# Two halves of a transposed row block placed between matmuls one by one, and the activation split moved ahead of the next weights at one seam of a two-block kernel

## The chip, the cores and the metric

The program runs on one core of one Trainium2 chip. The metric is the device time of one execution in microseconds (us). The engines are named as in the profile: PE is the matrix engine (PEld its weight loads), DVE the vector engine, ACT the scalar engine, POOL and SP the two others; SP issues the weight transfers.

## The reference

The input x is 256 tokens by 1024 columns. Two blocks follow each other, each of depth 2, all in float32:

```
# first block, for l in range(2)
proj = x @ w_in[l]                      # retention, mLSTM, gates
y_ret, y_ml = ..., ...                  # two sequence mixers, each with its own projection
mix = (gate_a * y_ret + gate_b * y_ml) @ w_out[l]
x = layer_norm(ALPHA * x + mix, ln1_g[l], ln1_b[l])
gu = x @ w_gate_up[l]
hidden = silu(gu[..., :D_FF]) * gu[..., D_FF:]
x = layer_norm(ALPHA * x + hidden @ w_down[l], ln2_g[l], ln2_b[l])

# second block, for l in range(2)
proj = rms_norm(h, norm_gain[l]) @ w_in_2[l]      # h starts as the x of the first block
y = ...                                           # dilated attention, stick-breaking attention, a gated recurrence
h = h + y @ w_out_2[l]
return rms_norm(h, final_gain)
```

Every projection needs the normalized activation with its columns on the partitions, while the normalization leaves it with tokens on the partitions. So after each normalization the kernel transposes the whole 256 by 1024 activation on PE.

## The kernel before, in words

**Split operands.** Each float32 product is made of three matmuls in a reduced float32 type: high weight by high activation, low weight by high, high weight by low. A weight unit is four blocks of 128 rows by 512 columns. SP loads it into `raw`; ACT copies it to `wh` (line 937, the high part); DVE subtracts to get `wl` (line 1362 for a unit or its second half, line 1373 for its first half alone). Rings of four `wh` and four `wl` buffers run ahead of PE. The activation is split in the same way: `xh` by ACT (line 973) and `xl` by DVE (line 1448), both read from the PSUM bank that PE transposed into, half of the 1024 columns at a time.

**Order.** There is no scheduler. Each engine has its program written out by hand, in the order of the projections (`mv0`, `mv1`, ..., `out0`, `out1`, `ff0`, ..., `dn1`, then `q`, `k`, ..., `o1` in the second block). Each engine works through its list in that order and waits on semaphores. On PE almost every matmul is issued from the helper at line 463; transposes of the normalized activation are at line 596.

**The seams.** The last projection ahead of a normalization is run by `by_half`: it first finishes token half t = 0 and then t = 1, so that the normalization of t = 0 lies beside the matmuls of t = 1. The normalized rows of t = 0 are transposed by `turn_x` between the last matmuls of t = 1. Behind it `pair` runs two projections together: t = 0 of both first, then t = 1; within the second one's first unit, at its third 128-row block (kk = 2), `turn_x` transposes the rows of t = 1. `turn_x` has two column halves, q = 0 and q = 1, each of four 128 by 128 transposes into one bank, and each waits for its half of the normalized row. `pair` meets its third unit in two halves on DVE: line 1373 makes the first half of `wl` before the normalization of t = 1 and line 1362 the second half behind it; PE waits for the second half at kk = 2.

In the first block this happens at `out1` and the pair `ff0`/`ff1` in both layers, and at `dn1` of layer 0 and the pair `mv0`/`mv1` of layer 1. **The passage** from the first block to the second is `dn1` of layer 1, followed by the pair `q`/`k`. There the rows pass two normalizations: X (lines 1621 to 1659, a layer norm), then squares on ACT (line 1100), a root on POOL (line 418) and the scaled rows `sg` (line 1642), which are transposed. In the second block the pair `q`/`k` of layer 1 follows the projection `o0`/`o1`, which calls `turn_x` for t = 0 in one piece before and after the change.

Of the kernel before, what the change touches and what calls it, by code (L numbers as in the profile page):

```python
# [13 lines left out]
P = 128  # L14
S = 256
D = 1024
DEPTH = 2
# [4 lines left out]
ALPHA = (2 * DEPTH) ** 0.25  # L22
LN_EPS = 1e-5
# [185 lines left out]
def program(nc, A, out):  # L209
# [8 lines left out]
    with top:  # L218
# [13 lines left out]
        X = sb("X", [P, 2, D])  # L232
# [220 lines left out]
        def tensor(pe):  # L453
# [90 lines left out]
            def half_k(t, bank, lh, ll, ready, k, unit, last, mid=None, mid_at=2):  # L544
                u, nk, h_, l_ = unit
                for kk in range(nk):
                    if mid and kk == mid_at:
                        mid()
                    if t == 0 and kk in (0, nk // 2):
                        pe.wait_ge(s_lo, 2 * u + 1 + (kk > 0))  # L550
                    ready(k + kk, t)
                    r = tok3(bank[:, :], lh, ll, k + kk, t, h_[:, kk, :], l_[:, kk, :], k + kk == 0)
                if t == 1:
                    r.then_inc(s_used, 1)
                elif last:
                    r.then_inc(s_half, 1)

            def by_half(name, l, head, tail, lh, ll, ready, mid, mid_at=3):
                k = 0
# [30 lines left out]
            def turn_x(l, tag, t, v, src, seen):  # L590
                for q in range(2):
                    name = f"{tag}{t}{q}"
                    bank, fill = open_aux(name, l)
                    pe.wait_ge(seen, v + 2 * t + q + 1)
                    for g in range(4):
                        r = pe.transpose(bank[:, tok_half(g)], src[:, P * (4 * q + g):P * (4 * q + g) + P], ident)  # L596
                    r.then_inc(fill, 1)
# [138 lines left out]
            for l in range(DEPTH):  # L736
                xw = x_whole(2 * l)
                one = lambda name, lh, ll, ready, mode, nu=2: group(SIDE1, steps, name, l, nu, lh, ll, ready, mode)
                if l == 0:
                    one("mv0", xh, xl, xw, "tok", 5)  # L740
                    one("mv1", xh, xl, xw, "tok")
                else:
                    pair("mv0", "mv1", l, x_part(2), lambda: turn_x(0, "xb", 1, 4, X[:, 1, :], s_xn), nothing, nothing)
# [15 lines left out]
                by_half("out1", l, 0, 2, mxh, mxl, mix_ready(l), lambda: turn_x(l, "xa", 0, 8 * l, X[:, 0, :], s_xn))  # L759
                pair("ff0", "ff1", l, x_part(2 * l + 1), lambda: turn_x(l, "xa", 1, 8 * l, X[:, 1, :], s_xn),  # L760
# [4 lines left out]
                if l == 0:  # L765
                    by_half("dn1", l, 4, 2, hdh, hdl, hidden_ready(l), lambda: turn_x(0, "xb", 0, 4, X[:, 0, :], s_xn), 3)
                else:
                    by_half("dn1", l, 3, 3, hdh, hdl, hidden_ready(l), lambda: turn_x(1, "xb", 0, 0, xn(0), s_rm), 2)
# [135 lines left out]
            for l in range(DEPTH):  # L904
                tag, at = ("xb", 1) if l == 0 else ("2x", 0)
                one = lambda name, mode: group(SIDE2, steps2, name, l, 2, xh, xl, x_whole(4 + l), mode)
                pair("q", "k", l, x_part(4 + l), lambda: turn_x(at, tag, 1, 4 * l, xn(1), s_rm), nothing, nothing)
# [5 lines left out]
                project(l, nothing if l == DEPTH - 1 else lambda: turn_x(0, "2x", 0, 4, xn(0), s_rm))  # L913
            assert use == NU

        def scalar(act):
# [186 lines left out]
            def by_half(name, l, head, tail, evac, mid):  # L1103
# [6 lines left out]
                for i in range(tail):  # L1110
                    if i == tail - 1:
                        mid()
                    highs(use - tail + i + 1 + RING)
# [29 lines left out]
            for l in range(DEPTH):  # L1143
# [35 lines left out]
                else:  # L1179
                    by_half("dn1", l, 3, 3, lambda t: squares(t, 4, [(s_xn, 12 + 2 * t + c + 1) for c in range(2)]),  # L1180
                            lambda: split_x("xb", l, 0, 4))
# [159 lines left out]
        def vector(dve):  # L1341
# [345 lines left out]
            def by_half(name, l, head, tail, evac, mid):  # L1687
# [9 lines left out]
                evac(0)  # L1697
                lows(high)
# [3 lines left out]
                mid()  # L1702
# [61 lines left out]
            for l in range(DEPTH):  # L1764
# [32 lines left out]
                by_half("dn1", l, 4 - l, 2 + l, lambda t: normal(l, "dn1", t, ALPHA, LN_EPS, 2 * l + 2), lambda: split_x("xb", l, 0, 2 * l + 2))  # L1797
# [209 lines left out]
```

## Time and profile before

| | |
|---|---|
| time, median of 3 runs | 1179.17 us (1177.88 to 1179.58) |
| profiled execution, its own time | 1179.37 us |
| span of the profiled execution | 1177.5 us |
| PE busy | 1160.3 us (99% of the span) |
| DVE, ACT, POOL busy | 741.8, 570.4 and 26.2 us |

The span runs from the first to the last instruction of the profile; 1.9 us of the time lie around it. The ends of matmuls are modelled by the profiler and overlap, so on PE the starts are what can be compared: a row's start less the start of the row ahead of it.

### The profile page before, as it was taken

The page shows a single profiled execution, that of the slowest core. Times are in us where ns is not written, and L with a number is a line of the kernel's source. Part 1 is how long each engine was busy: PE and PEld are TensorE (multiplying, and loading weights), DVE is VectorE, ACT ScalarE, POOL GpSimd, SP SyncE. Part 2 cuts the span into 40 slices and gives each one's busy share as a digit, 9 for nine tenths or more (in the row PEclk, how much of TensorE's full clock was granted, in tenths as well). Part 3 has the DMA queues.
Part 4 walks back from the last instruction along what each step waited for, and adds up shares of the span by engine and source line. Part 5 has one row for each costly group of instructions (what it writes and reads, how often), then busy time and mean ns, then how long its engine had stood idle before and what let it go on. Part 6 is the DMA issues. An engine that isn't in the chain of part 4 may idle for free.

```text
span 1177.5 us, 18016 instructions
## 1 busy us (share of the span) xinstructions
PE 1160.3 (99%) x7546; PEld 1042.4 (89%) x7546; DVE 741.8 (63%) x994; ACT 570.4 (48%) x658; POOL 26.2 (2%) x36
## 2 busy tenths in 40 slices
PE   8999999999999999999999999999999899999997
PEld 6988998998999988998998898899988689978995
DVE  5877556667655546686764667755545666775674
ACT  5563445442544434454444534444432556845673
POOL 0000000001000000000000000000000000000000
PEclk9999999999999999999999999999999999999999
DMA  9664454556665563745545556665566363336420
GB/s 343 220 215 144 144 181 176 180 186 201 224 212 190 167 212 112 250 151 172 170 144 189 179 179 214 230 208 182 169 203 208 125 215 128 127 138 243 137 80 36
DMA packets 129871, 211.45 MB, mean 180 GB/s; under 512 B 6528, under 2 KB 52608, under 8 KB 129664
## 3 DMA queue, kind: packets, MB, share of 16 engines
q1 hardware_dynamic: 128048, 204.02, 51.9%
q0 software_dynamic: 1744, 6.29, 1.8%
q8 instruction: 60, 0.98, 0.3%
q14 instruction: 19, 0.16, 0.0%
HBM read 209.24 MB, written 1.05 MB: 179 GB/s over the span
## 4 chain that ended last, share of the span: by engine, by line
PE 89%; DVE 5%; ACT 3%; DMA 2%; issue 1%; SPq 0%; POOL 0%; DVEq 0%; POOLq 0%; ACTq 0%
PE ps L463 85%; DMA raw<-in_w_in 2%; DVE wl L1362 1%; ACT wh L937 1%; PE ps L656 1%; PE ps L691 1%; PE ps L794 0%; DVE mqk L1490 0%; PE ps L596 0%; ACT sg L1100 0%; ACT xh L973 0%; DVE sg L1642 0%; PE ps L776 0%; PE ps L663 0%; DVE yl L1832 0%
## 5 line engine op out<-in xcount | busy, mean ns | idle before, releaser
L1362 DVE TENSOR_TENSOR wl<-raw,wh 128x2048 fp32r<-128x2048 f32 (+1 forms) x190 | 424.0, 2237 | 180.0 <-ACT wh L937 179.6
L937 ACT ACTIVATE wh<-raw 128x2048 fp32r<-128x2048 f32 (+1 forms) x190 | 359.9, 1900 | 181.0 <-PE ps L463 166.1
L463 PE MATMUL ps<-xh,wh 128*128 128x256 f32 x1200 | 337.1, 282 | 0.0
L463 PE MATMUL ps<-xl,wh 128*128 128x256 f32 x1200 | 332.1, 277 | 0.0
L463 PE MATMUL ps<-xh,wl 128*128 128x256 f32 x1184 | 328.4, 277 | 0.0
L463 PEld LDWEIGHTS ps<-xh,wh 128*128 128x128 f32 x1200 | 225.9, 188 | 3.2 <-issue 2.4
L463 PEld LDWEIGHTS ps<-xl,wh 128*128 128x128 f32 x1200 | 226.0, 188 | 0.4
L463 PEld LDWEIGHTS ps<-xh,wl 128*128 128x128 f32 x1184 | 222.6, 188 | 0.0
L463 PE MATMUL ps<-wh,xh 128*128 128x512 f32 (+1 forms) x512 | 203.8, 398 | 4.7 <-DVE wl L1362 2.4
L463 PE MATMUL ps<-wh,xl 128*128 128x512 f32 (+1 forms) x512 | 196.9, 385 | 0.0
L463 PE MATMUL ps<-wl,xh 128*128 128x512 f32 (+1 forms) x512 | 196.7, 384 | 0.0
L463 PEld LDWEIGHTS ps<-wh,xh 128*128 128x128 f32 x512 | 96.7, 189 | 26.8 <-DVE wl L1362 4.8
L463 PEld LDWEIGHTS ps<-wh,xl 128*128 128x128 f32 x512 | 96.5, 188 | 19.7
L463 PEld LDWEIGHTS ps<-wl,xh 128*128 128x128 f32 x512 | 96.8, 189 | 17.4
L463 PE MATMUL ps<-wh,hdh 128*128 128x512 f32 x176 | 68.7, 390 | 0.0
L463 PE MATMUL ps<-wl,hdh 128*128 128x512 f32 x176 | 68.5, 389 | 0.0
L463 PE MATMUL ps<-wh,hdl 128*128 128x512 f32 x176 | 68.5, 389 | 0.0
L1092 ACT ACTIVATE tmp<-ps 128x512 f32<-128x512 f32 x18 | 10.8, 598 | 63.5 <-PE ps L463 63.5
L463 PEld LDWEIGHTS ps<-wh,hdl 128*128 128x128 f32 x176 | 33.0, 188 | 6.9
L463 PEld LDWEIGHTS ps<-wh,hdh 128*128 128x128 f32 x176 | 33.0, 188 | 6.7
L463 PEld LDWEIGHTS ps<-wl,hdh 128*128 128x128 f32 x176 | 33.1, 188 | 6.7
L418 POOL TENSOR_TENSOR small<-small,cst 128x1 f32<-128x1 f32 (+1 forms) x18 | 17.9, 994 | 897.0 <-DVE small L1650 392.3
(259 smaller groups left out, 1384.6 us busy)
## 6 DMA issues: line engine op xcount, KB each, us to landing
raw<-in_w_in SPq DMA_DIRECT2D x90, 1024.0 KB, 5.1
raw<-in_w_gate_up SPq DMA_DIRECT2D x88, 512.0 KB, 4.9
raw<-in_w_down SPq DMA_DIRECT2D x20, 1024.0 KB, 4.9
raw<-in_w_out SPq DMA_DIRECT2D x16, 1024.0 KB, 5.0
raw<-in_w_proj_ret SPq DMA_DIRECT2D x8, 1024.0 KB, 4.9
raw<-in_w_proj_mlstm SPq DMA_DIRECT2D x8, 1024.0 KB, 5.0
rows<-in_ln_g POOLq DMA_DIRECT2D x4, 512.0 KB, 4.3
rows<-in_ln_b POOLq DMA_DIRECT2D x4, 512.0 KB, 5.7
```

What stands on the lines that cost most here:

```text
L418: pool.tensor_tensor(o, in_, C("mhalf", 0, n), ALU.pow).then_inc(after, 1)
L463: return pe.matmul(o, a, b, start=start, stop=False, skip_group_check=True)
L656: r = pe.matmul(bank[:, 0:257], dd_of(h)[:, o:o + P], mv[:, s, h, 0:257], start=(s == 0), stop=(s == t))
L691: r = pe.transpose(bank[:, S * k2 + P * t:S * k2 + P * t + P], src[:, t, tok_half(k)], ident)
L937: act.activation(stretch(wh, u, 0, m), source(u)[:, 0:m], ACT.Copy).then_inc(s_hi, 1)
L1092: act.activation(a_[:, :], main(name, l)[0][:, :], ACT.Silu).then_inc(freed_by(name, l, 0), 1)
L1362: dve.tensor_tensor(stretch(wl, u, a, nk * n), source(u)[:, a:nk * n], f32(stretch(wh, u, a, nk * n)), ALU.subtract).then_inc(s_lo, 1 if a ...
```

## The change

`turn_x` now does one column half, and `half_k` calls it twice: q = 0 ahead of block `mid_at`, q = 1 ahead of the next block, or behind the last block if there is no next one. In `by_half` of the first three seams q = 0 moves one block forward and q = 1 stays; in all pairs q = 0 stays and q = 1 moves one block back. At the passage both move back: q = 0 by one block, q = 1 to behind the last matmul of `dn1`. At the passage alone, ACT copies one weight unit instead of two before it makes `xh`, and DVE makes `xl` ahead of the next `wl` instead of behind it.

```diff
             def half_k(t, bank, lh, ll, ready, k, unit, last, mid=None, mid_at=2):
                 u, nk, h_, l_ = unit
                 for kk in range(nk):
-                    if mid and kk == mid_at:
-                        mid()
+                    if mid and kk - mid_at in (0, 1):
+                        mid(kk - mid_at)
                     if t == 0 and kk in (0, nk // 2):
                         pe.wait_ge(s_lo, 2 * u + 1 + (kk > 0))
                     ready(k + kk, t)
...
                 elif last:
                     r.then_inc(s_half, 1)
-
-            def by_half(name, l, head, tail, lh, ll, ready, mid, mid_at=3):
+                if mid and mid_at == nk - 1:
+                    mid(1)
+
+            def by_half(name, l, head, tail, lh, ll, ready, mid, mid_at=2):
...
-            def turn_x(l, tag, t, v, src, seen):
-                for q in range(2):
-                    name = f"{tag}{t}{q}"
-                    bank, fill = open_aux(name, l)
-                    pe.wait_ge(seen, v + 2 * t + q + 1)
-                    for g in range(4):
-                        r = pe.transpose(bank[:, tok_half(g)], src[:, P * (4 * q + g):P * (4 * q + g) + P], ident)
-                    r.then_inc(fill, 1)
+            def turn_x(l, tag, t, v, src, seen, q):
+                bank, fill = open_aux(f"{tag}{t}{q}", l)
+                pe.wait_ge(seen, v + 2 * t + q + 1)
+                for g in range(4):
+                    r = pe.transpose(bank[:, tok_half(g)], src[:, P * (4 * q + g):P * (4 * q + g) + P], ident)
+                r.then_inc(fill, 1)
...
-                    by_half("dn1", l, 4, 2, hdh, hdl, hidden_ready(l), lambda: turn_x(0, "xb", 0, 4, X[:, 0, :], s_xn), 3)
+                    by_half("dn1", l, 4, 2, hdh, hdl, hidden_ready(l), lambda q: turn_x(0, "xb", 0, 4, X[:, 0, :], s_xn, q))
                 else:
-                    by_half("dn1", l, 3, 3, hdh, hdl, hidden_ready(l), lambda: turn_x(1, "xb", 0, 0, xn(0), s_rm), 2)
+                    by_half("dn1", l, 3, 3, hdh, hdl, hidden_ready(l), lambda q: turn_x(1, "xb", 0, 0, xn(0), s_rm, q), 3)
...
-            def by_half(name, l, head, tail, evac, mid):
+            def by_half(name, l, head, tail, evac, mid, mid_after=None):
...
-                    if i == tail - 1:
+                    if i == (tail - 1 if mid_after is None else mid_after):
                         mid()
...
-                            lambda: split_x("xb", l, 0, 4))
+                            lambda: split_x("xb", l, 0, 4), 1)
...
-            def by_half(name, l, head, tail, evac, mid):
+            def by_half(name, l, head, tail, evac, mid, mid_first=False):
...
                 evac(0)
+                if mid_first:
+                    mid()
                 lows(high)
                 for i in range(tail - 1):
                     lows(high)
                     highs(use - tail + i + 1 + RING)
-                mid()
+                if not mid_first:
+                    mid()
                 raise_high(use + RING)
                 first_half_low()
```

The first place is DVE at the passage, before and then after: `sg` is the scaled row of t = 0, `xl` its low part, `wl` the low part of weights, `X<-X,ps` the first step of the normalization of t = 1.

```order
L1642 SCALAR_TENSOR_TENSOR sg<-X,small,rows 128x512
L1362 TENSOR_TENSOR wl<-raw,wh 128x2048 [waits s_hi]
L1448 TENSOR_TENSOR xl<-ps,xh 128x4x128 [waits s_xh,s_fill2]
L1448 TENSOR_TENSOR xl<-ps,xh 128x4x128 [waits s_xh,s_fill3]
L1373 TENSOR_TENSOR wl<-raw,wh 128x1024 [waits s_hi]
L1621 SCALAR_TENSOR_TENSOR X<-X,ps 128x512 [waits s_used]
```

```order
L1642 SCALAR_TENSOR_TENSOR sg<-X,small,rows 128x512
L1448 TENSOR_TENSOR xl<-ps,xh 128x4x128 [waits s_xh,s_fill2]
L1448 TENSOR_TENSOR xl<-ps,xh 128x4x128 [waits s_xh,s_fill3]
L1362 TENSOR_TENSOR wl<-raw,wh 128x2048 [waits s_hi]
L1373 TENSOR_TENSOR wl<-raw,wh 128x1024 [waits s_hi]
L1621 SCALAR_TENSOR_TENSOR X<-X,ps 128x512 [waits s_used]
```

The whole `wl` unit went from ahead of the two `xl` to behind them; all six still stand ahead of the normalization of t = 1.

The second place is PE in the pair `q`/`k` behind the passage, at blocks kk = 2 and kk = 3 of k's first unit, before and then after; `cst` is the identity, and `[waits s_lo]` is the wait for the second half of that unit's `wl`.

```order
L596 MATMUL ps<-cst,sg 128x128 [waits s_rm,s_drain0]
L596 MATMUL ps<-cst,sg 128x128 x3
L596 MATMUL ps<-cst,sg 128x128 [waits s_rm,s_drain1]
L596 MATMUL ps<-cst,sg 128x128 x3
L463 MATMUL ps<-wh,xh 128x512 [waits s_lo]
L463 MATMUL ps<-wl,xh 128x512
L463 MATMUL ps<-wh,xl 128x512
L463 MATMUL ps<-wh,xh 128x512
```

```order
L596 MATMUL ps<-cst,sg 128x128 [waits s_rm,s_drain0]
L596 MATMUL ps<-cst,sg 128x128 x3
L463 MATMUL ps<-wh,xh 128x512 [waits s_lo]
L463 MATMUL ps<-wl,xh 128x512
L463 MATMUL ps<-wh,xl 128x512
L596 MATMUL ps<-cst,sg 128x128 [waits s_rm,s_drain1]
L596 MATMUL ps<-cst,sg 128x128 x3
L463 MATMUL ps<-wh,xh 128x512
```

Four of the eight transposes went from ahead of the wait for the weights to three matmuls behind it. The other pairs have the same order, with `X` in place of `sg` in the first block.

The third place is PE at the end of `dn1` at the passage, after the change: the three `hdh`/`hdl` rows are block kk = 3, the last of `dn1`, and the row with `xh` is the first matmul of `q`.

```order
L596 MATMUL ps<-cst,sg 128x128 [waits s_rm,s_drain2]
L596 MATMUL ps<-cst,sg 128x128 x3
L463 MATMUL ps<-wh,hdh 128x512
L463 MATMUL ps<-wl,hdh 128x512
L463 MATMUL ps<-wh,hdl 128x512
L596 MATMUL ps<-cst,sg 128x128 [waits s_rm,s_drain3]
L596 MATMUL ps<-cst,sg 128x128 x3
L463 MATMUL ps<-wh,xh 128x512 [waits s_drain2,s_lo,s_free0]
```

Before, all eight transposes stood ahead of block kk = 2, with six matmuls between them and `q`.

## Rows read from the trace of the kernel before

**Rows 1.** The page, part 1: busy us (share of span) and instructions.
```profile
PE 1160.3 (99%) x7546; PEld 1042.4 (89%) x7546; DVE 741.8 (63%) x994; ACT 570.4 (48%) x658; POOL 26.2 (2%) x36
```

**Rows 2.** Waits of PE: us in total, times, longest us.
```profile
PE ps L463 <- DVE wl L1362: 2.4, 3, 1.5
PE ps L596 <- DVE sg L1642: 2.2, 2, 1.7
PE ps L463 <- DVE xl L1448: 2.1, 4, 0.8
```

**Rows 3.** Timeline, out1 of layer 0: start, us, engine, what [idle before].
```profile
277.08 1.41 DVE L1659 SCALAR_TENSOR_TENSOR X<-X,small,rows 128x512 f32<-128x512 f32 x2
...
278.56 1.03 PE L596 MATMUL ps<-cst,X 128*128 128x128 f32 x8
279.20 1.09 ACT L973 ACTIVATE xh<-ps 128x512 fp32r<-128x512 f32 x2 [0.50 <-PE ps L596]
...
279.89 1.29 DVE L1448 TENSOR_TENSOR xl<-ps,xh 128x512 fp32r<-128x512 f32 x2 [1.40 <-ACT xh L973]
...
280.73 0.47 PE L463 MATMUL ps<-wh,xh 128*128 128x512 f32 x1 [0.44 <-DVE xl L1448]
```

**Rows 4.** Timeline, pair ff0/ff1 of layer 0.
```profile
286.64 1.22 DVE L1362 TENSOR_TENSOR wl<-raw,wh 128x1024 fp32r<-128x1024 f32 x1
...
287.66 1.03 PE L596 MATMUL ps<-cst,X 128*128 128x128 f32 x8
...
288.45 0.48 PE L463 MATMUL ps<-wh,xh 128*128 128x512 f32 x1
...
289.91 0.39 PE L463 MATMUL ps<-wh,xh 128*128 128x512 f32 x1
```

**Rows 5.** Timeline at the passage, end of dn1 to start of q.
```profile
914.26 3.70 ACT L937 ACTIVATE wh<-raw 128x2048 fp32r<-128x2048 f32 x2
...
915.46 1.42 DVE L1642 SCALAR_TENSOR_TENSOR sg<-X,small,rows 128x512 f32<-128x512 f32 x2 [0.73 <-POOL small L418]
915.48 0.39 PE L463 MATMUL ps<-wh,hdl 128*128 128x512 f32 x1
...
916.35 1.29 PE L596 MATMUL ps<-cst,sg 128*128 128x128 f32 x8 [0.49 <-DVE sg L1642]
916.79 2.29 DVE L1362 TENSOR_TENSOR wl<-raw,wh 128x2048 fp32r<-128x2048 f32 x1
...
918.99 1.28 DVE L1448 TENSOR_TENSOR xl<-ps,xh 128x512 fp32r<-128x512 f32 x2
...
919.82 0.47 PE L463 MATMUL ps<-wh,xh 128*128 128x512 f32 x1 [0.80 <-DVE xl L1448]
...
920.19 1.21 DVE L1373 TENSOR_TENSOR wl<-raw,wh 128x1024 fp32r<-128x1024 f32 x1
...
921.32 0.68 DVE L1621 SCALAR_TENSOR_TENSOR X<-X,ps 128x512 f32<-128x512 f32 x1
```

**Rows 6.** Timeline in the pair q/k behind the passage.
```profile
928.57 1.29 PE L596 MATMUL ps<-cst,sg 128*128 128x128 f32 x8 [1.69 <-DVE sg L1642]
...
930.27 0.79 PE L463 MATMUL ps<-wh,xh 128*128 128x512 f32 x1 [0.41 <-DVE wl L1362]
...
930.87 0.63 PE L463 MATMUL ps<-wl,xh 128*128 128x512 f32 x1
...
932.57 0.63 PE L463 MATMUL ps<-wh,xl 128*128 128x512 f32 x1
```

**Rows 7.** Windows: stretch, us, busy by engine (x), PEclk, DMA share, GB/s.
```profile
930.00:931.00 1.00, 0.72 (x2) 0.63 (x3) 1.00 (x3) 0.49 (x1) 0.00 (x0) 0.50 0.33 49
...
933.00:934.00 1.00, 1.00 (x5) 0.85 (x4) 0.62 (x1) 0.00 (x0) 0.00 (x0) 0.83 0.93 285
```

**Rows 8.** Timeline, pair q/k of layer 1 of the second block.
```profile
1054.57 1.03 PE L596 MATMUL ps<-cst,sg 128*128 128x128 f32 x8
...
1055.75 0.19 PEld L463 LDWEIGHTS ps<-wh,xh 128*128 128x128 f32 x1 [0.39 <-DVE wl L1362]
```

More of the change, by code:

```diff
@@ L742, in tensor @@
                 else:
-                    pair("mv0", "mv1", l, x_part(2), lambda: turn_x(0, "xb", 1, 4, X[:, 1, :], s_xn), nothing, nothing)
+                    pair("mv0", "mv1", l, x_part(2), lambda q: turn_x(0, "xb", 1, 4, X[:, 1, :], s_xn, q), nothing, nothing)
                 gate(l)
@@ L758, in tensor @@
                 one("out0", mxh, mxl, mix_ready(l), "tok")
-                by_half("out1", l, 0, 2, mxh, mxl, mix_ready(l), lambda: turn_x(l, "xa", 0, 8 * l, X[:, 0, :], s_xn))
-                pair("ff0", "ff1", l, x_part(2 * l + 1), lambda: turn_x(l, "xa", 1, 8 * l, X[:, 1, :], s_xn),
+                by_half("out1", l, 0, 2, mxh, mxl, mix_ready(l), lambda q: turn_x(l, "xa", 0, 8 * l, X[:, 0, :], s_xn, q))
+                pair("ff0", "ff1", l, x_part(2 * l + 1), lambda q: turn_x(l, "xa", 1, 8 * l, X[:, 1, :], s_xn, q),
                      lambda: hidden_turn(l, 0, 0), lambda: hidden_turn(l, 0, 1))
@@ L906, in tensor @@
                 one = lambda name, mode: group(SIDE2, steps2, name, l, 2, xh, xl, x_whole(4 + l), mode)
-                pair("q", "k", l, x_part(4 + l), lambda: turn_x(at, tag, 1, 4 * l, xn(1), s_rm), nothing, nothing)
+                pair("q", "k", l, x_part(4 + l), lambda q: turn_x(at, tag, 1, 4 * l, xn(1), s_rm, q), nothing, nothing)
                 one("av", "tok")
@@ L912, in tensor @@
                 values_and_gates(l)
-                project(l, nothing if l == DEPTH - 1 else lambda: turn_x(0, "2x", 0, 4, xn(0), s_rm))
+                project(l, nothing if l == DEPTH - 1 else lambda: [turn_x(0, "2x", 0, 4, xn(0), s_rm, q) for q in range(2)])
             assert use == NU
@@ L1796, in vector @@
                 one("dn0", lambda: first_columns(l, "dn0", ALPHA), 6)
-                by_half("dn1", l, 4 - l, 2 + l, lambda t: normal(l, "dn1", t, ALPHA, LN_EPS, 2 * l + 2), lambda: split_x("xb", l, 0, 2 * l + 2))
+                by_half("dn1", l, 4 - l, 2 + l, lambda t: normal(l, "dn1", t, ALPHA, LN_EPS, 2 * l + 2), lambda: split_x("xb", l, 0, 2 * l + 2), l == 1)
             def rope(l):
```

## The prediction

> **What bounds the kernel now.** I read the page first: PE is busy 1160.3 of 1177.5 us [rows 1], so time can only be won in PE's few gaps or by taking work off PE, and the change takes none off. The waits of PE come next: three of them belong to the seams the change touches, 2.4 us for `wl`, 2.2 us for `sg` and 2.1 us for `xl` [rows 2]. The timelines then show where they lie. The four waits for `xl` are 0.80 us at the passage [rows 5] and three times about 0.44 us, one of them at `out1` of layer 0 [rows 3]; 0.80 + 3 x 0.44 is the 2.1 us. The waits for `sg` are 0.49 us ahead of the transposes of t = 0 [rows 5] and 1.69 us ahead of those of t = 1 [rows 6]. Everything outside these seams is matmul after matmul and is not touched.
>
> **Prices.** Eight transposes take PE 287.66 to 288.45, 0.79 us, so four take 0.40 us. A warm 512-column matmul takes 0.23 us: 30 of them lie between 280.73 and 287.66 [rows 3, 4]. The six behind the eight transposes take 1.46 us instead of 1.38 [rows 4], so a return from transposes to matmuls costs 0.08 us, and each half that is set apart costs 0.48 us of PE in place of 0.40. The hops are: first transpose to `xh` 0.64 us, `xh` to `xl` 0.69, `xl` to the matmul that needs it 0.84 [rows 3].
>
> **The three seams of the first block, t = 0.** At `out1`, the first half of X is ready in the middle of the two L1659, at 277.79. PE saw `sg` 0.18 us after its first half was ready (915.46 + 0.71 to 916.35) [rows 5], so q = 0 could start at 277.97, close to where kk = 2 started (278.56 less 3 x 0.23 = 277.87). Then 0.48 + 0.69 + 0.48 + 0.69 brings PE to 280.31. The data side is ready earlier, at 277.97 + 0.64 + 0.69 + 0.84 = 280.14. PE starts the next projection at 280.31 instead of 280.73: 0.42 us won.
>
> **The pairs behind them, t = 1.** The gain meets the next wait. PE would come to the transposes at 287.24, do four until 287.72, and then need the second half of `wl`, which DVE finishes at 286.64 + 1.22 = 287.86 [rows 4]. Before, the eight transposes covered that to the end. DVE gets to it through the normalization of t = 1, which starts no earlier: DVE's second `xl` ends where it did (277.97 + 1.17 for the second transposes, + 0.64 + 0.69 = 280.47, against 279.89 + 0.60 = 280.49). So kk = 2 starts at about 287.9, then 0.69 + 0.1 for the restart, 0.48, 0.69: the t = 1 pass starts at 289.8 instead of 289.91. Of 0.42 us about 0.1 is left. The third seam and the one in layer 1 show the same waits, so I take 3 x 0.1 = **-0.3 us**, with bounds of -1.3 (3 x 0.42 kept) and +0.3 (nothing won, three more returns at 0.08).
>
> **The passage, t = 0.** PE issued the last matmul of kk = 1 at 915.48 and then stood for `sg`. Now kk = 2 comes first, and q = 0 starts at 915.48 + 4 x 0.23 = 916.40, q = 1 at 916.40 + 0.48 + 0.69 = 917.57. `xh` starts at 917.04 and 918.21 (ACT is free, since one weight copy of 1.85 us from 914.26 ends at 916.1 [rows 5]), `xl` at 917.73 and 918.90. So `q` starts at 917.73 + 0.84 = 918.57 instead of 919.82: 1.25 us won on PE for the moment.
>
> DVE pays for it. Before, it went from `sg` (916.88) straight through `wl`, both `xl` and half of the next `wl` to X at 921.32, without a gap [rows 5]: `wl` filled the time in which transposes and `xh` were made. Now it waits from 916.88 to 917.73 and again between the two `xl`. The starts follow: `wl` at 918.90 + 0.60 = 919.50, the half `wl` 2.20 us later (918.99 less 916.79) at 921.70, X 1.13 us later (921.32 less 920.19) at 922.83. The normalization of t = 1 starts **1.51 us** later. PE first meets the late `wl`: 12 matmuls from 918.57 end at 921.3 and `wl` ends at 919.50 + 2.29 = 921.8, half a microsecond of waiting. Then it runs out of matmuls before the transposes of t = 1, and these wait for the chain from X, which took 921.32 to 928.57 [rows 5, 6] and is not shortened: they start at 930.08 instead of 928.57. The wait of 1.69 us becomes about 3.8. The won 1.25 us is swallowed in it, and the 1.51 us remain. Bounds: 0 below, since DVE had no idle time to give back and X cannot start before 921.32; 1.9 above, if each of the two DVE waits is 0.2 us longer (the hop of `sg` to PE again).
>
> Rows and a rule can be weighed here. At `out1` DVE stood idle for 1.40 us before `xl` although the weights of the next operation were there [rows 3]: a waiting instruction keeps those behind it back. The Trainium skill, TensorE: Matmul & The Clock Gate, section "Architectural detail", says the same of DVE and ACT, strict first in, first out. A DVE that let `wl` pass the waiting `xl` would make this term 0 and the time 1180.0; row and rule give 1181.5.
>
> **The passage, t = 1.** Before, all eight transposes lay in the time in which the second half of `wl` was made; PE went on when that was there, at 930.27 [rows 6]. Now four of them come three matmuls later, with nothing to hide them: **+0.48 us**, at the low clock more like 0.9; at the least 0.
>
> **The pair q/k of layer 1.** Here too PE waited 0.39 us for the second half of `wl` behind the eight transposes [rows 8]. Four move out of the covered time: **+0.48 us**, or 0 if they found cover. Its t = 0 part is unchanged.
>
> **Sum.** -0.3 + 1.51 + 0.48 + 0.48 = +2.2 us on the profiled execution's own 1179.37 us (span 1177.5 and 1.9 around it): **1181.5 us**. The profiled execution lies 0.2 us above the median, less than the terms' uncertainty. SP's loads and the copies behind the late `wl` are off the path: the weights they refill are used a whole ring later.
>
> **The clock.** Behind the two waits of rows 6 the granted clock stood at 0.50, the lower level of 1.2 GHz, and came back during the microsecond from 933 (0.83: a third of it low) [rows 7]. Matmuls went at (932.57 - 930.87) / 4 = 0.425 us; from 930.27 to 933.34 these are seven, 0.195 us dearer each, 1.4 us in all. That loss is in the time before; I keep it the same after.
>
> **Rivals.**
> 1. The clock stays low longer. PE's first wait more than doubles and a second of 1.2 us follows it, so the low stretch may begin earlier and outlast the restart by more, or the transposes run in it. Price up to another 1.4 us: 1182.9. It decides if the matmuls after the restart are slow for more than 3.1 us. The Trainium skill's same page, part 1, says that the low rate is the default and that activity lifts it, which speaks for it; that the low stretch ended while PE worked without a pause [rows 6, 7] agrees.
> 2. The clock doesn't fall. The four transposes now break the wait at another point. 1181.5 - 1.4 = 1180.1. The fastest run before, 1177.88, lies 1.3 us under the median, about this price, so such executions may exist; against it, the wait is longer.
> 3. The seams' gains are kept in full: 1181.5 - 1.0 = 1180.5. It needs the second half of `wl` 0.3 us earlier in the pairs, and DVE's chain gives no reason.
> 4. The 1.25 us at the passage are kept. It needs X to start at 921.32 or before and the chain behind it to have slack: 1179.37 - 1.25 - 0.3 + 0.48 = 1178.3. The rows speak against it, DVE being full from 915.46 to 921.32.
> 5. The order doesn't matter, because the halves reach `xh` together anyway: 1179.4. The order of the instructions speaks against it.
>
> **How the numbers follow.** Chances: my forecast 0.49 (1180.8 to 1182.3), clock longer 0.20, clock up 0.13, seams in full 0.08, passage kept 0.07, nothing 0.03. Dropping the far tails leaves 1178.6 to 1183.5. A measurement of this kernel can tell about 0.2%, 2.36 us, from no change; against the median that is 1181.5, where my forecast stands. Half of it and rival 1 are slower: 0.43. The other half with rivals 2 to 5 is no change: 0.53. Faster needs rival 4 with rivals 2 and 3 on top, 1175.9: 0.04.
>
> **What would show it.** Right: in the profile after, the waits of 0.44 us for `xl` at the three seams are gone and new waits for `wl` of 0.1 to 0.3 us stand in the pairs; at the passage DVE is idle before each `xl`, X of t = 1 starts 7.4 us after the first `sg` of t = 0 instead of 5.9 (921.32 less 915.46), and PE's wait for the `sg` of t = 1 is near 3.8 us. Wrong: X of t = 1 starts no later relative to `sg` of t = 0, or the transposes of t = 1 are not what PE waits for.

## The result, and the profile after

The changed kernel takes **1185.53 us** (median of 10 executions, 1181.86 to 1191.06) against 1179.01 for the kernel before (10 executions, 1177.88 to 1179.58): a ratio of 1.0052, interval [1.0041, 1.0063]. It is slower, and by more than forecast: 1181.5 us was expected, and the measured median lies above the range, which ended at 1183.5 us. The single times are also spread over 9.2 us where those of before span 1.7. The profiled execution is the slowest of the ten, 1191.06 us, span 1189.2.

The page's busy time of PE, which answers to [rows 1], and the waits of PE (total us, times, longest us), which answer to [rows 2]:

```profile
PE 1169.5 (98%) x7546; PEld 1050.7 (88%) x7546; DVE 742.8 (62%) x994; ACT 570.7 (48%) x658; POOL 26.2 (2%) x36
```

```profile
PE ps L463 <- DVE wl L1362: 4.0, 8, 1.4
PE ps L596 <- DVE sg L1642: 3.9, 1, 3.9
PE ps L463 <- DVE xl L1448: 0.4, 1, 0.4
```

The waits moved as forecast: those for `xl` went from four to one, those for `wl` from three to eight, and those for `sg` are now one long one. Yet the three together grew by 1.6 us only, while PE is busy 9.2 us longer with the same 7546 instructions. So most of the loss is in no wait at all.

**Where it lies.** The 6800 main matmuls (line 463) come in the same order in both kernels, so their starts can be compared one by one. In the profiled execution the changed kernel has lost 1.4 us by the second projection, where it waits for the first weights (that differs by as much and more between the profiles of the other kernels, whose instructions are the same up to there); it wins 0.2 us at the three seams and pairs, loses **3.5 us in `ff2` to `ff10` of each layer**, 3.2 us at the passage and 0.4 us at the pair q/k of layer 1. Less some 0.15 us of smaller steps this is the 11.7 us by which the spans differ.

**The seams and pairs.** The timeline at `out1` and the pair behind it, where [rows 3, 4] are those of before:

```profile
278.39 1.41 DVE L1659 SCALAR_TENSOR_TENSOR X<-X,small,rows 128x512 f32<-128x512 f32 x2
...
279.29 0.63 PE L596 MATMUL ps<-cst,X 128*128 128x128 f32 x4
...
281.58 0.40 PE L463 MATMUL ps<-wh,xh 128*128 128x512 f32 x1
...
289.20 0.50 PE L463 MATMUL ps<-wh,xh 128*128 128x512 f32 x1 [0.20 <-DVE wl L1362]
...
290.00 0.60 PE L596 MATMUL ps<-cst,X 128*128 128x128 f32 x4
```

The matmul at 281.58 has no wait where that of before had 0.44 us, and the pair has the new wait for `wl`, 0.20 us.

**The ff stage.** In `ff2` to `ff10` the activation is what moves: 864 matmuls of 256 columns, one behind the other. The first matmul of the stage, three neighbours in the middle of it and the first of `dn0` behind it, in the changed kernel and then in the kernel before:

```profile
305.27 0.28 PE L463 MATMUL ps<-xh,wh 128*128 128x256 f32 x1
...
350.17 0.28 PE L463 MATMUL ps<-xh,wh 128*128 128x256 f32 x1
350.29 0.28 PE L463 MATMUL ps<-xl,wh 128*128 128x256 f32 x1
350.40 0.28 PE L463 MATMUL ps<-xh,wl 128*128 128x256 f32 x1
...
407.41 0.39 PE L463 MATMUL ps<-wh,hdh 128*128 128x512 f32 x1
```

```profile
304.06 0.28 PE L463 MATMUL ps<-xh,wh 128*128 128x256 f32 x1
...
350.30 0.28 PE L463 MATMUL ps<-xh,wh 128*128 128x256 f32 x1
350.42 0.28 PE L463 MATMUL ps<-xl,wh 128*128 128x256 f32 x1
350.53 0.28 PE L463 MATMUL ps<-xh,wl 128*128 128x256 f32 x1
...
402.66 0.40 PE L463 MATMUL ps<-wh,hdh 128*128 128x512 f32 x1
```

From first to last row this is 102.14 us against 98.60. No row has a wait, and no instruction is added: the matmuls start 117.8 ns apart instead of 113.3. (Two decimals of a microsecond cannot show this between neighbours; it is the mean over the last 816 of the stage.) This distance from start to start is called the pitch below. The granted clock is not the reason. The windows of the changed kernel (stretch, us, busy by engine, PEclk, DMA share, GB/s) show PE full and the clock at 1.00:

```profile
305.00:355.00 50.00, 50.00 (x426) 49.92 (x425) 26.64 (x20) 22.68 (x20) 0.00 (x0) 1.00 0.68 219
```

In this window PE starts 426 matmuls; in the same 50 us of before it starts 442.

**The passage**, where [rows 5, 6] are those of before:

```profile
923.57 1.41 DVE L1642 SCALAR_TENSOR_TENSOR sg<-X,small,rows 128x512 f32<-128x512 f32 x2 [0.72 <-POOL small L418]
...
925.84 0.69 DVE L1448 TENSOR_TENSOR xl<-ps,xh 128x512 fp32r<-128x512 f32 x1 [0.85 <-ACT xh L973]
...
926.67 0.47 PE L463 MATMUL ps<-wh,xh 128*128 128x512 f32 x1 [0.44 <-DVE xl L1448]
...
926.97 0.69 DVE L1448 TENSOR_TENSOR xl<-ps,xh 128x512 fp32r<-128x512 f32 x1 [0.44 <-ACT xh L973]
...
930.91 0.68 DVE L1621 SCALAR_TENSOR_TENSOR X<-X,ps 128x512 f32<-128x512 f32 x1
...
938.15 0.63 PE L596 MATMUL ps<-cst,sg 128*128 128x128 f32 x4 [3.87 <-DVE sg L1642]
...
939.86 0.80 PE L463 MATMUL ps<-wh,xh 128*128 128x512 f32 x1 [1.08 <-DVE wl L1362]
...
941.31 1.05 PE L596 MATMUL ps<-cst,sg 128*128 128x128 f32 x4
...
945.15 0.60 PE L463 MATMUL ps<-wl,xh 128*128 128x512 f32 x1
945.57 0.41 PE L463 MATMUL ps<-wh,xl 128*128 128x512 f32 x1
```

Reckoned from `sg`, `q` starts after 3.10 us instead of 4.36, X of t = 1 after 7.34 instead of 5.86, and the transposes of t = 1 after 14.58 instead of 13.11. DVE stands still for 0.85 and 0.44 us ahead of the two `xl`.

### The profile page after: what moved, and what is told of

Read it like the earlier page. It is cut to its first block, busy times and chain, and to the rows that moved or that the text cites. A ratio compares the mean times of both kernels' runs of the same rounds, so it can differ in the third digit from the quotient of the medians.

```text
span 1189.2 us, 18016 instructions
## 1 busy us (share of the span) xinstructions
PE 1169.5 (98%) x7546; PEld 1050.7 (88%) x7546; DVE 742.8 (62%) x994; ACT 570.7 (48%) x658; POOL 26.2 (2%) x36
## 4 chain that ended last, share of the span: by engine, by line
PE 87%; DVE 6%; ACT 2%; DMA 2%; issue 1%; SPq 0%; POOL 0%; DVEq 0%; POOLq 0%; ACTq 0%
PE ps L463 84%; DVE wl L1362 2%; DMA raw<-in_w_in 2%; PE ps L656 1%; ACT wh L937 1%; PE ps L596 1%; PE ps L691 1%; PE ps L794 0%; DVE X L1659 0%; DVE mqk L1490 0%; DVE wl L1373 0%; SPq L402 0%; DVE sg L1642 0%; PE ps L663 0%; PE ps L776 0%
```

## The experiments

Each diff is against the kernel before, cut to its core. For the pitch, the table behind the second group gives the distance of neighbouring starts between breaks.

**First: which part brings the 118 ns.** Four kernels, each with one part of the change.

The passage alone (PE, ACT and DVE as in the change; PE's part shown):

```diff
-                    by_half("dn1", l, 3, 3, hdh, hdl, hidden_ready(l), lambda: turn_x(1, "xb", 0, 0, xn(0), s_rm), 2)
+                    by_half("dn1", l, 3, 3, hdh, hdl, hidden_ready(l), lambda q: turn_x(1, "xb", 0, 0, xn(0), s_rm, q), 3)
```

> Only the passage is changed (both halves of t = 0 later at the end of dn1 of layer 1, ACT and DVE in the new order); all other seams and pairs stand as before. In the trace of the change ff2 to ff10 go at 118 ns a matmul instead of 113, 3.53 us more in each layer, and the passage costs some 3.15 us. Theory PHASE (the 118 ns come from the way in which PE enters the stage, so from the splits at out1 and the pair ff0/ff1): both ff stages here at 113 ns, 98.5 us from first to last start, and the time 1179.0 + 3.15 = 1182.2 us. Theory OUTSIDE (the pitch is a state of the execution or of the weight transfers, and any kernel can fall into it): 118 ns here too in some of the executions, single times of 1185.7 and 1189, as with the whole change. My forecast's terms for the passage alone, with the clock loss as before and k unsplit: 1179.0 + 1.5 = 1180.5 us. The waits as forecast: sg of t = 1 near 3.8 us.

Measured: 1181.25 us, ratio 1.0016 [1.0007, 1.0025]; ff at 113 ns in both layers, no time above 1182.11. PE's wait for `sg` of t = 1 is 3.83 us, X starts 7.34 us after `sg`. That is 1.8 us more than before in its set, where +1.5 was forecast. In the profiled execution the transposes of t = 1 come 1.47 us later, and 0.64 us of it came back because the clock rose sooner behind them. The passage brings no 118 ns.

The first block alone: seams and pairs as in the change, passage and q/k as before.

```diff
-                by_half("out1", l, 0, 2, mxh, mxl, mix_ready(l), lambda: turn_x(l, "xa", 0, 8 * l, X[:, 0, :], s_xn))
-                pair("ff0", "ff1", l, x_part(2 * l + 1), lambda: turn_x(l, "xa", 1, 8 * l, X[:, 1, :], s_xn),
+                by_half("out1", l, 0, 2, mxh, mxl, mix_ready(l), lambda q: turn_x(l, "xa", 0, 8 * l, X[:, 0, :], s_xn, q))
+                pair("ff0", "ff1", l, x_part(2 * l + 1), lambda q: turn_x(l, "xa", 1, 8 * l, X[:, 1, :], s_xn, q),
```

> Only the first block is changed: q = 0 one block earlier at out1 of both layers and dn1 of layer 0, q = 1 one block later in the three pairs; the passage and the pairs q/k stand as before. PHASE: the seams win 0.3 us as forecast, and the ff stages fall to 118 ns in one or both layers in many executions: 1178.7, 1182.2 or 1185.8 us, so a median near 1182 and a spread of several us where the kernel before has 1.7. OUTSIDE: the same spread could show, but it would show in the passage kernel as well. If the pitch comes with the passage or with the program's length, 1178.7 us without a spread. Passage: PE's wait for sg of t = 1 stays 1.7 us.

Measured: 1178.4 us, 0.9994 [0.9985, 1.0003], 113 ns in both layers, single times 1177.65 to 1179.92. By the trace the three seams with their pairs win 0.14 us together. No execution fell to 118 ns here, against what I had expected of PHASE; the third group comes back to it.

The three seams alone: the pairs call both halves ahead of kk = 2, as before.

```diff
-                by_half("out1", l, 0, 2, mxh, mxl, mix_ready(l), lambda: turn_x(l, "xa", 0, 8 * l, X[:, 0, :], s_xn))
+                by_half("out1", l, 0, 2, mxh, mxl, mix_ready(l), lambda q: turn_x(l, "xa", 0, 8 * l, X[:, 0, :], s_xn, q))
```

> Only the three seams are split (q = 0 one block earlier at out1 of both layers and dn1 of layer 0); all pairs do their eight transposes in one piece, as before. By the rows, PE comes 0.42 us earlier to the pair, and the eight transposes (0.79 us) cover the time until the second half of wl is there, so the gain is kept: 1179.0 - 3 x 0.42 = 1177.8 us if ff stays at 113 ns. PHASE: PE enters the ff stage at another instant but behind the same instructions; if the instant against the data side decides, 118 ns in some layers (+3.53 us each: 1181.3 or 1184.8); if the order of PE's last instructions decides, 113 ns and 1177.8. OUTSIDE: 1177.8 with a spread of 3.5 us steps.

Measured: 1177.69 us, 0.9990 [0.9981, 0.9999], 113 ns. By the starts each seam wins 0.49 to 0.55 us, and no pair waits for `wl`: the eight transposes cover it. This part of the change is worth having.

The pairs alone, with both halves in one piece at the seams, as before.

```diff
-                pair("ff0", "ff1", l, x_part(2 * l + 1), lambda: turn_x(l, "xa", 1, 8 * l, X[:, 1, :], s_xn),
+                pair("ff0", "ff1", l, x_part(2 * l + 1), lambda q: turn_x(l, "xa", 1, 8 * l, X[:, 1, :], s_xn, q),
```

> Only the three pairs of the first block are split (q = 1 one block later); the seams ahead of them stand as before. PE reaches the pair as before, four transposes last 0.48 us and the second half of wl is there 0.2 us after the first of them began, so no wait is new and only the second return from transposes to matmuls is added, 0.08 us each: 1179.0 + 0.25 = 1179.3 us if ff stays at 113 ns. PHASE: the pair's new order shifts PE's entry into ff2 by some nanoseconds: 118 ns in one or both layers, 1182.8 or 1186.3 us. OUTSIDE: 1179.3 us with steps of 3.5 us in single executions.

Measured: 1185.47 us, 1.0062 [1.0048, 1.0075], all five times from 1184.81 to 1188.4, and **118 ns in both layers**. Three transposed halves that move by three matmuls, with no wait added, cost 6 us in a stage 15 us further on (by the starts 7.1 us in the two stages; 1.4 us came back behind the passage, where the clock did not fall in the profiled execution).

**Second: the breaks.** In the ff stage of all these traces the pitch changes only behind the small transposes of the hidden rows, two 128 by 128 transposes that stand twice in `ff2`. A kernel with one break more was the test, first on the split pairs, then on the kernel before with nothing of the change.

```diff
+            def extra_turn(l, j, t):
+                bank, fill = open_aux(f"f{j}{t}", l)
+                main_done(f"ff{j}", l, t)
+                for k in range(2):
+                    pe.transpose(bank[:, tok_half(k)], tmp[2 + t][:, tok_half(k)], ident)
-    "ff2": (("f 1 0",), ("f 1 1",), (), ()),
+    "ff2": (("f 1 0",), ("x 1 1",), ("f 1 1",), ()),
```

> The kernel with only the pairs of the first block split went at 118 ns in ff2 to ff10 of both layers, 1185.47 us, and its trace changes pitch just behind the two small transposes that ff2 holds: 118 ahead of the first pair of them, 113 between, 118 behind the second. Here one further pair of the same transposes (into the same bank, written over by the next) stands in ff2, in both layers. PHASE (the pitch is carried from matmul to matmul and is set anew by each break in the row of matmuls): the third break sets it anew, most simply back to 113: 1185.5 - 7.0 + 2 x 0.3 for the added transposes = 1179.1 us; that it stays at 118 is possible too, since the kernel before shows a break that left it there. OUTSIDE (a state of the execution, or of the transfers, or of what this pair order loads): 118 all the same, 1185.5 + 0.6 = 1186.1 us.

Measured: 1186.9 us, 1.0068 [1.0056, 1.0080]; it stayed at 118.

> The kernel before, with nothing of the change, and the same further pair of small transposes in ff2 of both layers: four transposes in all. The trace of before has 118 ns ahead of and behind the first break and 113 behind the second. PHASE: the third break sets the pitch anew, and ff2 to ff10 go at 118 ns: 1179.3 + 2 x (3.5 + 0.3) = 1186.9 us. If so, the 7 us can be had without any part of the change. OUTSIDE: 113 as in before, 1179.3 + 0.6 = 1179.9 us.

Measured: 1186.6 us, 1.0062 [1.0050, 1.0074], and 118 ns in both layers. First matmul of `ff2` and first of `dn0` in its timeline:

```profile
305.96 0.28 PE L463 MATMUL ps<-xh,wh 128*128 128x256 f32 x1
...
408.32 0.39 PE L463 MATMUL ps<-wh,hdh 128*128 128x512 f32 x1
```

102.36 us: two transposes of some 0.2 us cost 3.8 us a layer. The loss can be had without the change.

These sequences suggested a cycle, and a fourth break on the split pairs tested it (`"x 1 1"` stands in two places of `ff2`):

```diff
-    "ff2": (("f 1 0",), ("f 1 1",), (), ()),
+    "ff2": (("f 1 0",), ("x 1 1",), ("x 1 1",), ("f 1 1",)),
```

> The pairs of the first block split, as in the kernel that gave 1185.47 us, with two further pairs of small transposes in ff2 instead of one, so four breaks in all. Read from four traces, each break of two transposes takes the row of matmuls one step on in a cycle of three, 118, 118, 113 and 118 again: the kernel before comes in at the first and has 118, 118, 113; with a further break 118, 118, 113, 118; the split pairs come in at the second and have 118, 113, 118; with a further break 118, 113, 118, 118. Theory CYCLE: here 118, 113, 118, 118, 113, so ff3 to ff10 go at 113 ns in both layers: 1185.5 - 2 x (3.5 - 0.7) = 1179.9 us, with 0.25 us for each added pair of transposes and some matmuls more at 118. Theory ORDER (the split pair order itself gives 118, and added transposes can only add): 118 behind the last break, 1185.5 + 4 x 0.25 = 1186.5 us.

Measured: 1180.23 us, 1.0011 [1.0002, 1.0019], 113 ns in both layers, 0.3 us from the forecast of CYCLE. Its two rows:

```profile
307.24 0.28 PE L463 MATMUL ps<-xh,wh 128*128 128x256 f32 x1
...
406.45 0.40 PE L463 MATMUL ps<-wh,hdh 128*128 128x512 f32 x1
```

99.21 us with two breaks more, where the same kernel with one more had 102.4. The mean distance of starts in each piece between breaks (from the tenth matmul of a piece on, the same in both layers):

| kernel | ns ahead of the first break, then behind each |
|---|---|
| before; seams alone; passage alone; first block alone (both sets) | 117.8, 117.8, **113.3** |
| before with one break more | 117.8, 117.8, 113.3, **117.8** |
| changed, profile of the result; pairs alone | 117.8, 113.3, **117.8** |
| changed, profiles of two further sets (third group) | 117.8, 117.8, **113.3** |
| pairs alone with one break more | 117.8, 113.3, 117.8, **117.8** |
| pairs alone with two breaks more | 117.8, 113.3, 117.8, 117.8, **113.3** |

Each break of two transposes takes one step in the cycle 118, 118, 113; the kernels differ in the step at which they come in. The last piece is 768 to 816 matmuls long, and 816 x 4.45 ns = 3.6 us.

**Third: the whole change again**, and beside it the first block alone.

> The whole change once more, beside the other kernels on one chip. Its PE does up to 912 us the same in the same order as the kernel with only the first block changed, which stood at 113 ns and 1178.4 us in all its executions. PHASE: which of the two it gets is decided by the nanosecond at which DVE's wl releases PE in the pair (445 ns from matmul to matmul there in the one, 468 in the other), so it can differ from execution to execution and from chip to chip: single times in groups near 1181.0, 1184.6 and 1188.1 us, for none, one or two layers at 118 ns, and the profiled one has the pitch that its time says. If the whole change fixes the pitch: all near 1185.5 to 1188.

Measured: 1185.98 us, 1.0059 [1.0039, 1.0079], times 1181.7, 1182.74, 1185.4, 1186.56, 1189.02 and 1189.93. The profiled execution is the one of 1181.7 us, and both its layers are at 113 ns. So the same program has both pitches.

> The kernel with only the first block changed again, now on the same chip as the whole change. It had 113 ns in all its executions (1177.65 to 1179.92 us), the whole change in the two other sets 113 or 118 from execution to execution, although PE does the same up to 912 us in both. CHIP (the release that decides falls differently on different chips, or from set to set): single times in groups near 1178.5, 1182 and 1185.5 us here too, or none in both kernels. KERNEL (something in the rest of the change moves that release by nanoseconds): all near 1178.5 us here, mixed in the whole change beside it.

Measured: 1179.61 us, 1.0011 [1.0001, 1.0022]; five of twelve times lie above all of before's in that set (1180.96 to 1184.7). The theory KERNEL, that this program always has 113, falls by these times alone: the profiled execution is at 113, and no profile caught this program at 118.

> The whole change beside the kernel with only the first block changed, on one chip. CHIP: the same mix of layers at 113 and 118 ns as there. KERNEL: single times in groups near 1181.5, 1185 and 1189 us again (so far 5, 8 and 3 of 16), while the other stays at 1178.5. In the profiled execution the release of PE by wl in the pair ff0/ff1, reckoned back from the first matmul of ff2, tells the pitch: 16.068 to 16.069 us back went with 118, 16.078 to 16.113 with 113 in six layers.

Measured: 1183.28 us, 1.0045 [1.0032, 1.0057], times 1182.56 to 1187.48; profiled the one of 1182.56, at 113 ns in both layers. Its release by `wl` lies 16.079 us ahead of `ff2` in both layers, on the side that the expectation gave to 113; no further profile at 118 came to test the other side.

The two kernels in whose pairs PE stands for `wl` between the two halves of the transposes are mixed, one of them by its times only; in the kernels without that wait every profile had the pitch of its row in the table.

The record has the same at a second place. Near 39 us PE waits for `hml`, does four small matmuls and then 96 matmuls of 256 columns in a row. PE's instructions up to there are the same in all kernels here, yet the row goes at 113 ns in nine of the 16 profiles and at 118 ns in seven. The second matmul of the row and the 89th behind it, in the kernel before and then with the pairs alone:

```profile
39.00 0.28 PE L463 MATMUL ps<-xl,wh 128*128 128x256 f32 x1
...
49.10 0.28 PE L463 MATMUL ps<-xh,wh 128*128 128x256 f32 x1
```

```profile
39.37 0.28 PE L463 MATMUL ps<-xl,wh 128*128 128x256 f32 x1
...
49.85 0.28 PE L463 MATMUL ps<-xh,wh 128*128 128x256 f32 x1
```

That is 10.10 us against 10.48. So the order of the instructions alone does not fix the pitch behind a wait. (Here it costs next to nothing: what the faster row wins, PE loses behind it in a wait for `gb`, 0.34 us in the kernel before.)

**Fourth: the passage and q/k, taken apart.** DVE in the old order, the rest of the passage as in the change, all other seams and pairs as before:

```diff
-                by_half("dn1", l, 4 - l, 2 + l, lambda t: normal(l, "dn1", t, ALPHA, LN_EPS, 2 * l + 2), lambda: split_x("xb", l, 0, 2 * l + 2), l == 1)
+                by_half("dn1", l, 4 - l, 2 + l, lambda t: normal(l, "dn1", t, ALPHA, LN_EPS, 2 * l + 2), lambda: split_x("xb", l, 0, 2 * l + 2))
```

(this one against the changed kernel.)

> Of the change only the passage, and there PE's two later halves and ACT's earlier xh, but DVE in the old order, wl ahead of both xl. With xl first as well the passage alone gave 1181.25 us, and X of t = 1 started 7.3 us after sg. Theory DVE (the idle of DVE ahead of each xl is what pushes the normalization of t = 1 back): X starts 5.9 us after sg again, xl ends where it did before, q starts as before, and PE's wait for sg of t = 1 is back near 1.7 us: 1179.4 us. Theory PE (the halves set apart on PE cost the time): the time stays near 1181 us, with the wait for sg unchanged at some 3.8 us.

Measured: 1179.58 us, 1.0007 [0.9998, 1.0016]. In its timeline, where the line numbers are 6 higher:

```profile
915.93 1.41 DVE L1648 SCALAR_TENSOR_TENSOR sg<-X,small,rows 128x512 f32<-128x512 f32 x2 [0.73 <-POOL small L418]
...
921.05 1.22 DVE L1379 TENSOR_TENSOR wl<-raw,wh 128x1024 fp32r<-128x1024 f32 x1 [0.31 <-ACT wh L943]
922.20 0.68 DVE L1627 SCALAR_TENSOR_TENSOR X<-X,ps 128x512 f32<-128x512 f32 x1
...
929.45 1.75 PE L596 MATMUL ps<-cst,sg 128*128 128x128 f32 x8 [2.07 <-DVE sg L1648]
```

X starts 6.27 us after `sg`: 1.07 of the 1.48 us are gone with DVE's order. Of the 0.41 us that are left beyond before, 0.31 stand in the row of `wl` as a wait for `wh`: ACT, which now copies one unit of weights instead of two ahead of `xh`, comes to it later. Theory DVE holds for the larger part, with a share for ACT that I had not named; the row shows it, no run changed ACT's order by itself.

The pairs q/k alone:

```diff
-                pair("q", "k", l, x_part(4 + l), lambda: turn_x(at, tag, 1, 4 * l, xn(1), s_rm), nothing, nothing)
+                pair("q", "k", l, x_part(4 + l), lambda q: turn_x(at, tag, 1, 4 * l, xn(1), s_rm, q), nothing, nothing)
```

> Only the pairs q/k of the second block are split, in both layers; all else as before. The forecast's two terms by themselves: 0.48 us in layer 1 and 0.48 to 0.9 us behind the passage, where the four transposes that have moved may run at the lower level of the clock: 1179.2 + 1.0 to 1.4 = 1180.2 to 1180.6 us. Rival (the moved transposes find cover, because the rows behind them were ready early): 1179.2 us. ff at 113 ns in both layers in any case, since nothing ahead of it is changed.

Measured: 1179.11 us, 1.0005 [0.9995, 1.0015]. The time alone is inconclusive, its interval holds both theories. By the starts the profiled execution, 1180.47 us, loses 0.66 us behind the passage and 0.43 us in layer 1 against that of before, together the 1.1 us by which the two differ. The clock fell behind the passage in both, at different moments, so the 0.66 us are not the split alone.

**Fifth: the other stage, and a faster kernel.** `yr0` to `ym1` went at 118 ns in all kernels so far. Seams alone, and the last four transposes of `hml` in two breaks of two:

```diff
-    "yr0": (("om 0",), ("om 1",), ("om 2",), ("om 3",)),
+    "yr0": (("om 0",), ("om 1",), ("om 2",), ("oma 3",)),
+    "yr1": (("om 3",), (), (), ()),
...
-                for k2 in range(2):
+                for k2 in part:
...
-                r.then_inc(fill, 1)
+                if 1 in part:
+                    r.then_inc(fill, 1)
```

> The kernel with the three seams split alone (1177.69 us), and in yr0/yr1 of both layers the last four transposes of hml set in two breaks of two, one in the last place of yr0 and one at the first place of yr1; no transpose is added. In all kernels so far yr0 to ym1 went at 118 ns behind four breaks of four. CYCLE: if a break of two takes a step here too, two of them lead from the first 118 through the second to 113, and some 290 matmuls a layer go 4.4 ns faster: 1177.7 - 2 x 1.2 = 1175.3 us. If breaks act otherwise in this stage (other operands in other places of memory): 118 as before, 1177.7 + 0.2 = 1177.9 us.

Measured: 1177.96 us, 0.9988 [0.9979, 0.9997], no better than the seams alone. The trace has 117.8 up to the first of the two breaks, 113.3 for 24 matmuls, and 117.8 behind the second: a step in the cycle each, but this stage comes in one step later than I had assumed. So four breaks of two are needed:

```diff
-    "yr0": (("om 0",), ("om 1",), ("om 2",), ("om 3",)),
+    "yr0": (("om 0",), ("om 1",), ("oma 2",), ("om 2",)),
+    "yr1": (("oma 3",), ("om 3",), (), ()),
```

> The three seams split alone, and in yr0/yr1 of both layers the last two groups of four transposes of hml each set in two breaks of two. With the last group alone so divided the trace went 118, 113 for 24 matmuls, and 118 again behind the second break: the stage comes in at the second step of the cycle, and breaks of four leave the pitch where it is. CYCLE: four breaks of two take it from the second step over 113, 118, 118 to 113, which then holds for some 240 matmuls a layer: 46.8 to about 45.9 us from first to last start of the stage, 2 x 0.9 us off the kernel with the seams alone (1177.69 us, 1177.96 with the last group divided): 1175.9 us. If the agreement so far was chance: 118 behind the last break, 1177.9 us.

Measured: **1174.39 us, 0.9960 [0.9948, 0.9973]**, faster than both kernels. First matmul of `yr0`, two neighbours behind the fourth break, and the first of `out0`:

```profile
210.39 0.28 PE L464 MATMUL ps<-orh,wh 128*128 128x256 f32 x1
...
240.20 0.28 PE L464 MATMUL ps<-omh,wl 128*128 128x256 f32 x1
240.31 0.28 PE L464 MATMUL ps<-omh,wh 128*128 128x256 f32 x1
...
256.29 0.40 PE L464 MATMUL ps<-wh,mxh 128*128 128x512 f32 x1
```

45.90 us, where the kernel before has 46.98 (210.41 to 257.39 in its timeline):

```profile
210.41 0.28 PE L463 MATMUL ps<-orh,wh 128*128 128x256 f32 x1
...
257.39 0.40 PE L463 MATMUL ps<-wh,mxh 128*128 128x512 f32 x1
```

The last 240 matmuls are at 113.3 ns in both layers. The time is 1.5 us below the forecast. By the starts the profiled execution is 3.6 us ahead of that of before: 1.5 us at the three seams and 2.2 us in the two stages, less 0.2 us at the clock behind the passage. The medians differ by 4.6 us; the rest I leave to the spread of five executions.

## Why the prediction was wrong

**The step that failed** is a sentence of the first part: "Everything outside these seams is matmul after matmul and is not touched." The ff stage is touched: it costs 3.53 us more in a layer that goes at 118 ns, 7.1 us in the two. In all profiles its pitch follows from the step of a cycle of three at which PE comes out of the pair ahead of it, and the pair was changed. In the first four experiments only split pairs gave 118 ns; the kernel before with one break more has it without any part of the change, so breaks alone move the pitch, and two breaks more on the split pairs bring 113 ns back. None of the five rivals had it, so the range missed too. What in the machine makes the cycle is not shown by any run.

**The rest of the sum held, but for the clock.** The two profiled executions of the changed kernel in which ff kept 113 ns took 1181.7 and 1182.56 us; the forecast was 1181.5. By the starts, with the first 63 us and the ff stage left out, the three profiles of this kernel lose 3.3, 2.6 and 3.4 us against before, where the sum had 2.2. The surplus lies at the clock behind the passage, below.

| term | forecast, us | measured by starts, us |
|---|---|---|
| three seams with their pairs | -0.3 | -0.19 (changed, three profiles), -0.14 and -0.16 (first block alone) |
| a seam by itself | -0.42 | -0.49 to -0.55 (seams alone) |
| passage, t = 0 | +1.51 | +1.47 (14.58 less 13.11) |
| passage, t = 1, with the clock behind it | +0.48 to 0.9, clock as before | +0.66 (q/k alone); +1.71, +0.91, +1.65 (changed, three profiles) |
| pair q/k of layer 1 | +0.48 | +0.41 to +0.45 |
| ff stage | 0 | 0 or 7.1 in the profiles |

**The seams.** The working had the halves too dear: set apart, four transposes took PE 0.36 to 0.38 us up to the next matmul, not 0.48, so a seam wins 0.5 us and not 0.42. This gain meets the late second half of `wl`, as the working had it: PE waits 0.17 to 0.21 us for it in each pair, as forecast. Split seams with whole pairs keep the gain; with split pairs 0.01 to 0.09 us a seam is left, where 0.1 was forecast.

**The passage, t = 0.** The three signs asked for are in the rows: the two idle times of DVE (0.85 and 0.44 us), X 7.34 us after `sg` (forecast 7.4) and the wait for `sg` of 3.87 us (forecast 3.8). And `q` starts 3.10 us after `sg`, as the working had it (3.11). That a waiting instruction holds back what stands behind it, which the forecast took from the row at `out1` and for which it named the Trainium skill, is borne out by the kernel with DVE's old order, where 1.07 us go away. The working had one omission: by the row of that kernel, ACT's new order has 0.31 us in it.

**The clock.** The sum kept the clock's loss as it was before, and here it was too small. The sign of rival 1, matmuls slow for more than 3.1 us behind the restart, stands in all three profiles of the changed kernel. In that of the result the matmuls behind the wait went 0.43 us apart until 945.57, 5.7 us from the restart at 939.86, against 3.1 us before; in the two others the granted clock was back after 4.0 and 5.6 us. From the restart to the thirtieth matmul behind it PE took 10.06, 9.26 and 10.00 us, and 8.35 before. With the 1.47 us of t = 0 the first of these makes the 3.2 us at this place. Whether the change brings the longer stretch is not shown: it was 1.7 us with the passage alone and 4.0 us with q/k alone, and in the five other profiles with the passage as before in which the clock fell it was 2.5 to 3.7 us.

That the clock does not fall, rival 2, needs nothing of the change, and none of the three profiles shows it. Behind the same instructions in the same order, the matmuls at the lower level behind the first one number 6 in the profile of before and 7, 6, 8, 5 and 7 in these five; in four more kernels with that passage the clock stayed at 1.00. With the pairs alone the restart is at 937.80 (windows as above):

```profile
938.00:942.00 4.00, 4.00 (x18) 3.27 (x18) 3.14 (x3) 0.02 (x1) 0.00 (x0) 1.00 0.92 264
```

There the thirty matmuls took 6.97 us, 1.4 us less than in the kernel before, which is the price that the forecast worked out for the fall. The Trainium skill, TensorE: Matmul & The Clock Gate, part 1, says that the hardware's look at the activity runs free of the kernel, so that the moment of the change depends on where the kernel falls; the counts of 0 to 8 agree with this. A term of this kind belongs in the range, not in the sum.

**The size of the median.** Without the ff stage the terms as measured by the starts give 1179.0 + 2.6 to 3.4, so 1181.6 to 1182.4 us. One layer at 118 ns would add 3.5 us, two add 7.1. The 21 single times of the changed kernel, 1181.7 to 1191.06 us, fit a mixture of these, with the start's 1 to 2 us on top; but they do not fall into clear groups, and no profile has one layer alone at 118 ns. So 1185.53 is most likely a mixture, and another set gave 1183.28. What stays open is what in the release by `wl` decides: the first block alone was at 113 throughout one set and, by its times, mixed in another, and whether chip or execution makes that difference was not settled.

## What to carry to other kernels

A long run of equal matmuls can have one of two pitches, and which one can depend on what stands ahead of it. Before calling such a stage untouched, compare the starts of neighbouring matmuls in it in both traces, since neither waits nor the granted clock show it; and where the pitch has two values, look for a break that can be divided or joined to choose the better one. Moving a waiting instruction ahead of ready work holds that work back for the time of the wait, even where the consumer is served earlier: here `q` started 1.26 us sooner and the chain behind it 1.48 us later, of which the old order by itself took 1.07 back.

## What was unexpected of the hardware

The same matmuls (256 columns, weights loaded for each, clock 1.00) ran at 113.3 or 117.8 ns for 816 in a row, and a break of two transposes moved them from one to the other in the order 118, 118, 113. Breaks of four transposes in `yr0` left the pitch at 117.8 each time. The Trainium skill, TensorE: Matmul & The Clock Gate, section "Back-to-back issue gap", gives N / 2.4 + 2.5 ns as the gap of a single matmul of N columns at full clock. An estimate from that for 256 columns is 109 ns. The two measured values lie above it and differ by 4%, so for a stream like this the measurement decides.
